# Seven-product down projections in a two-block fp32 kernel, modulation loads issued by GpSimd, and a third buffer of probabilities

## The chip, the cores and the metric

The kernel runs on one core of one Trainium2 chip. The metric is the device time of one execution in microseconds, the median over runs. Everything is fp32.

## The reference, cut to what matters

Two transformer blocks run one after the other on 256 tokens of width 1024, each two layers deep. The change touches the first block's layers and the modulation vectors of the second block's first layer.

```
# first block, for layer in (0, 1)
xn = rms_norm(x, mix_norm[layer])
layer 0: mixed = fox_diff_mixer(...)      # 8 heads of forgetting attention, 4 of differential attention
layer 1: mixed = mlstm_mixer(...)
x = x + mixed
x = x + memory_cross_attention(rms_norm(x), rms_norm(mem), wq, wkv, wo)
h = causal_depthwise_conv(rms_norm(x) @ w_up, conv_w) + conv_b       # 1024 -> 2 x 2816
g, u = split(h);  x = x + (gelu(g) * u) @ w_down                     # 2816 -> 1024
# second block, before its first layer
mod  = silu(c)     @ w_mod[0] + b_mod[0]   # 6144 outputs from 1024 inputs
modc = silu(c_ctx) @ w_mod[0] + b_mod[0]
```

The modulation depends on c and c_ctx alone. It can be computed at any time before the second block.

## The kernel before

**Layout.** Activations are kept feature-major: X, XN and SQ are tiles of 128 features by 8 feature blocks by 512 columns, of which the first 256 are the tokens (T) and the second 256 are free in the first block, apart from keys and values of the memory. A large `arena` is carved into areas by hand. The weights come as one stream of slabs (2 to 2.8 MB each) into two slots; SyncE (SP) issues each slab's DMA when TensorE has finished the slab two before it (L2986). Every engine runs one fixed program, written part by part with `add(...)`; parts of one engine run strictly in the order in which they were added, and semaphores tie the engines together. So where a part stands in VectorE's order decides what waits behind it.

**Order of the stages in the first block, layer 0.** `memkv0` (keys and values of the memory), the norm `mixnorm0`, `foxgate` (forget gates, followed by `add_log_sigmoid` on ScalarE and VectorE and a scan), `foxin` (the input projection: 8 jobs of two 128-feature tiles over 256 tokens, then 4 token-major jobs), `fox` (the attention, `*_pairs`), `subln`, `mixout0`, `xq0`, `xatt0` (cross attention), `xo0`, `fnorm0`, `upa0`, `downa0`. Layer 1 ends likewise with `upa1` and `downa1`; the last layer of the second block ends with `downb1`.

**foxin.** Job j writes PSUM bank j mod 4. ScalarE reads jobs 0, 1, 4, 5; VectorE reads jobs 2, 3, 6, 7 (L2016, L1504). TensorE may start job j only when job j-4 has been read out of its bank (`claim`).

**The up projections** (`*_up_seven`) compute each pair of 128-feature tiles with seven products of quarters in place of eight (Strassen's scheme in Winograd's form), 22 blocks of which 16 run in a hardware loop of 4 turns.

**The down projections.** `downb0` and `downb1` use seven products (`*_down_seven`): for each pair of output tiles, 7 products of 11 k tiles, each over half of the tokens. GpSimd and VectorE form the sums of the weight quarters in the slot, VectorE forms four sums of the hidden activations once. `downa0` and `downa1` use the plain form (`add_out` to `tensor_linear`): 8 output tiles by 22 k tiles over 256 tokens. An fp32 matmul is two matmul instructions in the trace, so the plain form has 352 and the seven-product form 616.

**The modulation** has 48 tiles of 128 outputs. Each tile is a 512 KB piece of w_mod, transposed; VectorE multiplies it with silu(c) and sums along the row (L619, `tensor_tensor_reduce` of 128x1024), once for c and once for c_ctx, so 96 products. Before, 24 tiles are done in `upa0`/`downa0` and 24 in `upa1`/`downa1`: one per turn of the loop, one behind some of the last blocks, six between up and down, and the rest between the reads of the plain down projection. SP issues their loads among the slabs (L2992), with four buffers.

**The forgetting and differential attention** (`*_pairs`) has 8 units (4 pairs of forgetting heads, 4 differential heads). Per unit u: scores on TensorE; `minima(u)` on VectorE, which adds the mask, writes into the probabilities' buffer and takes the minimum; exponentials on ScalarE; `recip(u)`, the scaling (L1463); transposes `turn(u)` on TensorE (L1349); copies; values. VectorE's order is minima(u), recip and scaling of u-1, copy of u-2. There are two buffers, so minima(u) waits for turn(u-2), the last reader of the buffer.

Of the kernel before, what the change touches and what calls it, by code (L numbers as in the profile page):

```python
# [23 lines left out]
P = 128  # L24
# [229 lines left out]
def two_blocks(nc, x_in, mem_in, ctx_in, c_in, small_in, weights_in, mod_in, out, known):  # L254
# [6 lines left out]
    with ExitStack() as ctx:  # L261
# [4 lines left out]
        for n in ("tensor_done", "scalar_done", "vector_done", "gpsimd_done",  # L266
                  "landed0", "landed1", "mod_landed0", "mod_landed1", "mod_landed2", "mod_landed3", "late_landed0", "late_landed1", "loaded_c", "landed_first", "landed_second", "loaded_x", "loaded_mem0", "loaded_mem1", "loaded_mem2", "loaded_mem3", "loaded_ctx", "loaded_small", "loaded_rest",
                  "conv_done", "mod_done", "stored"):
            sems[n] = ctx.enter_context(nc.semaphore(n))
# [3 lines left out]
        CD, MD = "conv_done", "mod_done"  # L273
# [334 lines left out]
        MOD_LOOP, MOD_HALF = 4, MOD_TILES // 2  # L608

        def mod_slot(r):  # L610
            return 0 if r < MOD_LOOP else (r - MOD_LOOP + 1) % 4

        def mod_landed(f, r):

            before = [mod_slot(i) for _ in range(f) for i in range(MOD_HALF)] + [mod_slot(i) for i in range(r + 1)]
            return sems[f"mod_landed{mod_slot(r)}"], 16 * before.count(mod_slot(r))
# [4 lines left out]
        def vector_mod_turn(dve, s, g, turn):  # L621

            f = int(s[1])
            if g == 0:
                sem, landed = mod_landed(f, 0)
                dve.wait_ge(sem, landed + 16 * turn)
                dve.wait_ge(*of(s, "mod_kept", turn=turn, back=1))
            w = mod_slots[0]
            vector_mod_product(dve, w, MODC[:, g, :, :], tiny[:, 48 + g:49 + g], w if g else MODP)\
                .then_inc(*tick(MD, s, "mod_product", g))  # L630
            if g:
                dve.wait_ge(*of(s, "mod_product", 1, turn=turn))
                dve.tensor_copy(MOD[:, 0, bass.ds(turn + MOD_HALF * f, 1), :],
                                tiny[:, 48:50].rearrange("p (m g) -> p m g", g=2)).then_inc(*tick(MD, s, "mod_kept"))

        def vector_mod_tile(dve, s, r, g):
            f = int(s[1])
            w = mod_slots[mod_slot(r)]
            if g == 0:
                dve.wait_ge(*mod_landed(f, r))  # L640
                if r > MOD_LOOP:
                    dve.wait_ge(*of(s, "mod_tile", r - 1, 0))
            vector_mod_product(dve, w, MODC[:, g, :, :], MOD[:, 0, MOD_HALF * f + r, g:g + 1], w if g else MODP)\
                .then_inc(*tick(VD, s, "mod_tile", r, g))
# [169 lines left out]
        def scalar_up_seven(act, s, segs):  # L814
            n, _, centre = conv_spec(s[0], segs)
            h = n // 2
            if s[0] == "a":
                act.wait_ge(sems["loaded_c"], 16 * (int(s[1]) + 1))
                act.activation(MODC, MODC, ACT.Silu).then_inc(*tick(SD, s, "silu_c"))

# [29 lines left out]
        def vector_up_seven(dve, s, norm, segs):  # L850
# [49 lines left out]
            def body(i, turn, m):  # L900
# [111 lines left out]
        def tensor_down_seven(pe, s, pairs, n):  # L1012
# [4 lines left out]
            for p in range(pairs):  # L1017
# [38 lines left out]
                Stream.slab += 1  # L1056

        def vector_down_seven(dve, s, pairs, n, gate):
# [5 lines left out]
            def add_to_x(p, i, g, src):  # L1064
                m = 2 * p + i
                x = X[:, m, g * h:(g + 1) * h]
                return dve.scalar_tensor_tensor(out=x, in0=src, scalar=gate(m, g if n > T else 0), in1=x, op0=ALU.mult,
                                                op1=ALU.add)
# [4 lines left out]
            for p in range(pairs):  # L1073
# [54 lines left out]
                add_to_x(p, 0, 1, ps["p3"]).then_inc(*tick(VD, d, "read", 2 * p, 1))  # L1128

        def gpsimd_down_sums(pool, s, p):  # L1130
# [8 lines left out]
            if p == 0 and s == "b1":  # L1139
                return  # L1140
# [186 lines left out]
        PT = [PTR, RT]  # L1327

        def tensor_pairs(pe, s, units, ready, early=None, late=None):
# [13 lines left out]
            def turn(u):  # L1343
                un = units[u]
                for i in (1, 0):
                    claim(pe, 4 + i)
                    pe.wait_ge(*of(s, "probs", u, i))
                    for a, b in un["blocks"]:
                        mm = pe.transpose(PS[:, 4 + i, b:b + P], PR[:, 2 * (u % 2) + i, a:a + P], ident)  # L1349
# [29 lines left out]
        def scalar_pairs(act, s, units, early=()):  # L1379
            def exps(u):  # L1380
                un = units[u]
                act.wait_ge(*of(s, "min", u))
                if u >= 2:
                    act.wait_ge(*of(s, "turned", u - 2, 0))
                if u >= RING:
                    act.wait_ge(*of(s, "rec", u - RING))
                src = PS if un["rows"][0][2] is None else PR
                for i in range(2):
                    for j, (c0, c1, _) in enumerate(un["rows"]):
                        r = i * len(un["rows"]) + j  # L1390
                        op = act.activation(PR[:, 2 * (u % 2) + i, c0:c1], src[:, 2 * (u % 2) + i, c0:c1], ACT.Exp,
# [29 lines left out]
        def vector_pairs(dve, s, units):  # L1421
            def minima(u):
# [4 lines left out]
                if units[u]["rows"][0][2] is not None:  # L1427
                    if u >= 2:
                        dve.wait_ge(*of(s, "turned", u - 2, 0))
# [51 lines left out]
        def gpsimd_pairs(pool, s, units):  # L1481
            if s in ("fox", "batt0", "batt1"):
                return
# [1814 lines left out]
```

## Time and profile before

| | |
|---|---|
| median of 3 runs | 2523.35 us (2518.7 to 2523.64) |
| the profiled execution, its own time | 2517.16 us |
| its span | 2515.1 us |
| instructions | 36,716 |
| TensorE busy | 98% of the span |
| weights and other reads from memory | 331.72 MB, mean 132 GB/s |

The profile is one execution taken by the hardware profiler. Times in it are microseconds from the span's start. PE is TensorE's matmuls, PEld its weight loads, DVE is VectorE, ACT ScalarE, POOL GpSimd, SP SyncE. Matmuls are pipelined, and the end of a group is modelled, so distances between the starts of groups are read rather than durations. "idle before <- releaser" is the time the engine stood still before an instruction and who ended that. PEclk is the granted TensorE clock, where 1.00 is 2.4 GHz and 0.50 is 1.2 GHz.

### The profile page before, as it was taken

To read this page: it belongs to the slowest core of one execution; us is meant where nothing else is said; L and a number is where in the kernel's file an instruction comes from. 1 tells how busy PE (TensorE), PEld (TensorE's weight loads), DVE (VectorE), ACT (ScalarE), POOL (GpSimd) and SP (SyncE) were. 2 spreads that over 40 slices of the span, in tenths; PEclk is the share of its full clock that TensorE was granted. 3 is DMA by queue.
4 is the path that set the end of the run, shared out by engine and by line. 5 is a ranking of instruction groups with operands and counts; after the bars stand their busy time and mean duration, and the time that the engine had idled before them with its cause. 6 is when DMAs were issued, how large, how long until landed. Compare 5 with 4: busy or idle time off the path is not lost.

```text
span 2515.1 us, 36716 instructions
## 1 busy us (share of the span) xinstructions
PE 2475.1 (98%) x14000; PEld 2020.7 (80%) x14000; DVE 1270.1 (51%) x2602; ACT 544.5 (22%) x1198; POOL 550.1 (22%) x474
## 2 busy tenths in 40 slices
PE   9989999999999999999999999999999999999999
PEld 6857899986799998745567666888888875999999
DVE  3034178751325887324846763544542247435774
ACT  1131122111212220213630001222200215212220
POOL 1000135200212540001002321323241010232543
PEclk9999999999999999999999999999999999999999
DMA  6323265643334566121023662121222120243453
GB/s 236 134 101 117 84 226 186 261 180 134 117 134 168 193 226 234 67 81 39 1 84 142 222 252 104 67 100 67 113 92 80 67 94 26 104 167 150 167 193 109
DMA packets 40018, 334.59 MB, mean 133 GB/s; under 512 B 3920, under 2 KB 10192, under 8 KB 22736
## 3 DMA queue, kind: packets, MB, share of 16 engines
q1 hardware_dynamic: 39888, 332.78, 35.7%
q8 instruction: 91, 1.49, 0.2%
q14 instruction: 39, 0.32, 0.0%
HBM read 331.72 MB, written 1.05 MB: 132 GB/s over the span
## 4 chain that ended last, share of the span: by engine, by line
PE 92%; DVE 3%; DMA 3%; POOL 1%; ACT 1%; issue 1%; SPq 0%; DVEq 0%; POOLq 0%; ACTq 0%
PE PS L769 25%; PE PS L569 21%; PE PS L2763 6%; PE PS L1029 6%; PE PS L1529 6%; PE PS L1719 4%; PE PS L2804 4%; PE PS L1338 3%; PE PS L1704 3%; PE PS L2282 2%; PE PS L1349 2%; PE PS L1361 2%; DMA slot<-in_weights 2%; PE PS L436 1%; PE PS L750 1%; PE PS L2420 1%
## 5 line engine op out<-in xcount | busy, mean ns | idle before, releaser
L569 PE MATMUL PS<-XN,slot 128*128 128x256 f32 (+1 forms) x1184 | 296.8, 411 | 0.8 <-DVE XN L508 0.8
L769 PE MATMUL PS<-SQ,slot 128*128 128x128 f32 (+1 forms) x1984 | 294.5, 301 | 2.2 <-DVE slot L865 2.2
L569 PEld LDWEIGHTS PS<-XN,slot 128*128 128x128 f32 x1184 | 224.5, 190 | 69.9 <-issue 42.5
L769 PEld LDWEIGHTS PS<-SQ,slot 128*128 128x128 f32 x1984 | 268.1, 191 | 15.5 <-DVE slot L865 2.6
L769 PE MATMUL PS<-XN,slot 128*128 128x128 f32 (+1 forms) x1664 | 250.0, 301 | 0.0
L569 PE MATMUL PS<-arena,slot 128*128 128x256 f32 x1088 | 236.6, 379 | 0.8 <-DMA slot<-in_weights 0.7
L769 PEld LDWEIGHTS PS<-XN,slot 128*128 128x128 f32 x1664 | 226.1, 192 | 10.7
L569 PEld LDWEIGHTS PS<-arena,slot 128*128 128x128 f32 x1088 | 206.3, 190 | 30.8 <-issue 1.9
L892 DVE SCALAR_TENSOR_TENSOR arena<-PS,small,arena 128x255 f32<-128x255 f32 (+2 forms) x352 | 174.9, 544 | 47.3 <-ACT arena L836 47.1
L836 ACT ACTIVATE arena<-PS,small 128x256 f32<-128x256 f32 (+1 forms) x176 | 105.1, 616 | 376.3 <-DVE PS L925 237.6
L480 POOL TENSOR_TENSOR SQ<-SQ 128x512 f32<-128x512 f32 (+1 forms) x36 | 42.3, 1178 | 536.6 <-ACT SQ L446 536.1
L1029 PE MATMUL PS<-arena,slot 128*128 128x128 f32 (+1 forms) x846 | 130.6, 314 | 1.3 <-DVE arena L1103 0.8
L1029 PEld LDWEIGHTS PS<-arena,slot 128*128 128x128 f32 x846 | 119.9, 191 | 10.0 <-DVE arena L1103 1.0
L446 ACT ACTIVATE SQ<-X 128x512 f32<-128x512 f32 (+1 forms) x68 | 36.2, 551 | 410.3 <-DVE X L1642 172.2
L619 DVE CUSTOM_DVE_ANT_1 arena<-arena 128x1024 f32<-128x1024 f32 x96 | 121.2, 1312 | 3.7 <-DMA arena<-in_mod 3.7
L2763 PE MATMUL PS<-arena,slot 128*128 128x256 f32 (+1 forms) x704 | 119.6, 328 | 1.5 <-DVE slot L2887 1.4
L2763 PEld LDWEIGHTS PS<-arena,slot 128*128 128x128 f32 x704 | 107.0, 191 | 11.6 <-DVE slot L2887 2.2
L769 PE MATMUL PS<-SQ,probs 128*128 128x128 f32 (+1 forms) x704 | 111.4, 301 | 1.3 <-DVE SQ L877 1.3
L1719 PE MATMUL PS<-arena,slot 128*128 128x128 f32 (+1 forms) x688 | 110.1, 321 | 0.0
L950 POOL TENSOR_TENSOR slot<-slot 128x512 f32<-128x512 f32 x84 | 109.0, 1297 | 0.0
L1719 PEld LDWEIGHTS PS<-arena,slot 128*128 128x128 f32 x688 | 101.4, 191 | 8.4 <-issue 0.5
L962 POOL TENSOR_TENSOR arena<-arena 128x256 f32 (+3 forms) x88 | 79.8, 906 | 113.7 <-ACT arena L845 113.7
(291 smaller groups left out, 3661.8 us busy)
## 6 DMA issues: line engine op xcount, KB each, us to landing
slot<-in_weights SPq DMA_DIRECT2D x85, 2048.0 KB, 7.8
arena<-in_mod SPq DMA_DIRECT2D x96, 512.0 KB, 3.4
slot<-in_weights SPq DMA_DIRECT2D x16, 2816.0 KB, 9.7
slot<-in_weights SPq DMA_DIRECT2D x24, 1536.0 KB, 6.7
slot<-in_weights SPq DMA_DIRECT2D x5, 1024.0 KB, 4.8
slot<-in_weights SPq DMA_DIRECT2D x2, 2176.0 KB, 8.8
arena<-in_c SPq DMA_DIRECT2D x3, 1024.0 KB, 10.9
small<-in_small SPq DMA_DIRECT2D x1, 1982.0 KB, 17.2
```

The costliest lines, as they stand in the source:

```text
L569: mm = pe.matmul(o, l, r, start=k == 0, stop=k == len(terms) - 1, skip_group_check=True)
L619: return dve.tensor_tensor_reduce(scratch, w, c, 1.0, 0.0, ALU.mult, ALU.add, total)
L769: mm = pe.matmul(PS[:, bank, 0:h], lhs[:, k * P:(k + 1) * P], rhs(k), start=first and k == 0, stop=last and k == 3, skip_group_check=True)
L836: act.activation(hb[:, half, :], src[half], ACT.Identity, bias=conv_col(s, m - 1, half, 3), scale=conv_col(s, m - 1, half, centre))\
L892: op = dve.scalar_tensor_tensor(out=o[:, :, lo:hi], in0=x[:, :, lo + d:hi + d], scalar=conv_col(s, m - 1, half, c), in1=o[:, :, lo:hi], op ...
L950: pool.tensor_tensor(a21, a11, a21, ALU.subtract).then_inc(*w_tick(s, GD, "s3", i, turn))
L962: pool.tensor_tensor(dst, hb[:, 0, :], hb[:, 1, :], ALU.mult).then_inc(*w_tick(s, GD, "h", i, turn))
L1029: mm = pe.matmul(d_psum(p, what, h), lhs[:, k * P:(k + 1) * P], rhs(k), start=k == 0, stop=k == KH - 1, skip_group_check=True)
L1529: mm = pe.matmul(PS[:, bank, 0:cols_n], lhs(k, t), r, start=k == 0, stop=k == k_tiles - 1)
L1719: mm = pe.matmul(PS[:, bank_of(m), part[g]], w[:, a:a + P], rhs(k, part[g]), start=k == 0, stop=k == k_tiles - 1, skip_group_check=True)
L2763: mm = pe.matmul(PS[:, bank, 0:hq], lhs[:, k * P:(k + 1) * P], rhs[:, k, 0:hq], start=first and k == 0, stop=last and k == 3, skip_group_c ...
L2804: mm = pe.matmul(PS[:, BBR + i, 0:nq], slot[:, a:a + P], BR[b][:, k, 0:nq], start=k == 0, stop=k == 3, skip_group_check=True)
```

## The change

1. `downa0` and `downa1` use `*_down_seven`, with half the tokens (128 columns) per product, as `downb1` does. Nothing is gated there, so the addition to X is a plain addition. The context norm that was laid behind the first job of `downa1` is now laid behind its second pair.
2. All 48 modulation tiles move to layer 0 of the first block: tiles 0 to 7 right before `foxgate`'s read, 8 to 15 before the read of `foxin` job 2, 16 to 22 before that of job 6, 23 to 32 before the attention, 33 to 39 between the reads of `mixout0`, 40 to 47 between those of `xo0`. They have three buffers. Their loads are issued by GpSimd, each when the tile three before it is done, and no longer by SP. silu(c) is computed before tile 0 (in the free half of X) and once more before tile 40. The products inside the up stages and their loads between slabs are gone.
3. The attention `fox` has three buffers of probabilities: minima(u) waits for turn(u-3).

```diff
-        MODC = H[:, 0:DK, T:2 * T].rearrange("p (g j) t -> p g j t", g=2)
-        MODP = H[:, DK:DK + 4, T:2 * T]
-        mod_slots = [area(15360 + D * i, 4, T) for i in range(4)]
+        MODC = [X[:, :, T:2 * T].rearrange("p (g j) t -> p g j t", g=2), area(12288, 2, 4, T)]
+        mod_slots = [[area(at, 4, T) for at in (16384, 17408, third)] for third in (12288, 14592)]
+        MODP = area(18432, 4, T)
...
+        MOD_SLOTS, MOD_OUT, MOD_XO = 3, 35, 40
+        def vector_mod_tiles(dve, *tiles):
+            for n in tiles:
+                w = mod_slots[n >= MOD_OUT][n % MOD_SLOTS]
+                c = MODC[n >= MOD_XO]
+                if n in (0, MOD_XO):
+                    dve.wait_ge(*of("silu_c", int(n >= MOD_XO)))
+                dve.wait_ge(sems[f"mod_landed{n % MOD_SLOTS}"], 16 * (n // MOD_SLOTS + 1))
+                for g in range(2):
+                    if g == 0 and n:
+                        dve.wait_ge(*of("mod_tile", n - 1, 0))
+                    vector_mod_product(dve, w, c[:, g, :, :], MOD[:, 0, n, g:g + 1], w if g else MODP)\
+                        .then_inc(*tick(VD, "mod_tile", n, g))
+                if n % MOD_HALF == MOD_HALF - 1:
+                    vector_mod_end(dve, 0, n // MOD_HALF, [("mod_tile", n, 1)])
+        def gpsimd_mod_loads(pool, tiles):
+            for n in tiles:
+                if n == 2:
+                    pool.wait_ge(*of("memkv0", "job", 3))
+                if n == MOD_OUT:
+                    pool.wait_ge(*of("subln", "out", 3, 0))
+                if n >= MOD_SLOTS:
+                    pool.wait_ge(*of("mod_tile", n - MOD_SLOTS, 1))
+                pool.dma_start(mod_slots[n >= MOD_OUT][n % MOD_SLOTS], mod_in[n].rearrange("p (j t) -> p j t", t=T))\
+                    .then_inc(sems[f"mod_landed{n % MOD_SLOTS}"], 16)
+        def scalar_silu_c(act, f):
+            act.wait_ge(sems["loaded_c"], 16 * (f + 1))
+            act.activation(MODC[f], MODC[f], ACT.Silu).then_inc(*tick(SD, "silu_c", f))
...
-                if s[0] == "a" and turn is not None:
-                    if i == 0:
-                        dve.wait_ge(*of(s, "silu_c"))
-                    if i % 2 == 0:
-                        vector_mod_turn(dve, s, i // 2, turn)
-                elif s[0] == "a" and i >= W_LAST and i % 2 == 0:
-                    vector_mod_tile(dve, s, MOD_LOOP, (i - W_LAST) // 2)
...
-            if p == 0 and s == "b1":
+            if p == 0 and s != "b0":
                 return
...
+        PAIR_SETS = {t: [PR[:, 0:2, :], PR[:, 2:4, :]] for t in ("fox", "batt0", "batt1")}
+        PAIR_SETS["fox"].append(area(18432, 2, 512))
...
-                if u >= 2:
-                    act.wait_ge(*of(s, "turned", u - 2, 0))
+                if pair_before(s, u) >= 0:
+                    act.wait_ge(*of(s, "turned", pair_before(s, u), 0))
...
-            add_out(f"d{s}", lambda k: H[:, k, 0:T * len(segs)], None, FM, segs, gate,
...
+            add(tensor=lambda pe: tensor_down_seven(pe, s, DK // 2, n, tensor_then),
+                vector=lambda d: vector_down_seven(d, s, DK // 2, n, gate, vector_then),
+                gpsimd=lambda p: gpsimd_down_seven(p, s, DK // 2, n))
...
+                add(scalar=lambda a: scalar_silu_c(a, 0), vector=lambda d: vector_mod_tiles(d, *range(0, 8)),
+                    gpsimd=lambda p: gpsimd_mod_loads(p, range(0, MOD_OUT)))
...
+                def vector_foxin(dve, jobs=fox_jobs):
+                    for j, job in enumerate(jobs):
+                        vector_mod_tiles(dve, *{2: range(8, 16), 6: range(16, 23)}.get(j, ()))
+                        reads_linear(dve, VD, "vector", "foxin", [job], j)
+                    vector_mod_tiles(dve, *range(23, 33))
...
                 add_out("mixout0", lambda k: O1[:, k, :],
...
+                        [(33, 34), (35, 36, 37), (38, 39), ()])
...
+                add_out("xo0", lambda k: O1[:, k, :], lambda k: ("xatt0", "out", k // 2), DK, [0],
+                        [(40, 41, 42), (43, 44, 45), (46, 47), ()])
...
+            prev_ready = [[(f"da{l}", "read", 2 * p, 1)] for p in range(DK // 2)]
...
+                if g == 2:
+                    load_c(0)
+                if g == first_slab["mixout0"] + 1:
+                    sp.wait_ge(*of("subln", "out", 3, 0))
+                    load_c(1)
```

## Rows read from the trace of the kernel before

**Rows 1.** The page: busy time by engine; GpSimd's busy tenths in 40 slices
```profile
PE 2475.1 (98%) x14000; PEld 2020.7 (80%) x14000; DVE 1270.1 (51%) x2602; ACT 544.5 (22%) x1198; POOL 550.1 (22%) x474
...
POOL 1000135200212540001002321323241010232543
```

**Rows 2.** The page: the chain that ended last, shares by engine
```profile
PE 92%; DVE 3%; DMA 3%; POOL 1%; ACT 1%; issue 1%; SPq 0%; DVEq 0%; POOLq 0%; ACTq 0%
```

**Rows 3.** Waits of PE: total us, times, longest
```profile
PE PS L1349 <- DVE probs L1463: 6.1, 5, 1.6
...
PE PS L769 <- DVE slot L865: 2.2, 2, 1.1
```

**Rows 4.** PE in order: start, us, instructions, [idle before]
```profile
69.40 55.52 PE L569 MATMUL PS<-XN,slot 128*128 128x256 f32 x256
...
458.55 3.84 PE L769 MATMUL PS<-SQ,slot 128*128 128x128 f32 x32 [1.07 <-DVE slot L865]
...
470.26 76.14 PE L569 MATMUL PS<-arena,slot 128*128 128x256 f32 x352
...
2440.75 5.08 PE L1029 MATMUL PS<-arena,slot 128*128 128x128 f32 x44
...
2454.93 10.09 PE L1029 MATMUL PS<-arena,slot 128*128 128x128 f32 x88 [0.79 <-DVE arena L1103]
...
2501.71 9.99 PE L1029 MATMUL PS<-arena,slot 128*128 128x128 f32 x88
```

**Rows 5.** The chain that ended last, 440 to 475: start, us
```profile
444.11 8.92 DMA slot<-in_weights
```

**Rows 6.** DVE in order, foxgate to fox, then products and a read
```profile
69.50 0.47 DVE L2002 TENSOR_SCALAR arena<-PS,small 8x256 f32<-8x256 f32 x1 [1.21 <-PE PS L569]
...
73.17 0.68 DVE L2009 TENSOR_TENSOR_SCAN arena<-small,arena 8x256 f32<-8x256 f32 x1
...
118.05 0.69 DVE L1504 COPY arena<-PS 128x512 f32<-128x512 f32 x1 [20.03 <-PE PS L569]
...
156.24 0.29 DVE L1432 CUSTOM_DVE_ANT_0 probs<-PS,small 128x128 f32<-128x128 f32 x1 [30.59 <-PE PS L1338]
...
509.06 1.21 DVE L619 CUSTOM_DVE_ANT_1 arena<-arena 128x1024 f32<-128x1024 f32 x1
...
510.20 2.29 DVE L619 CUSTOM_DVE_ANT_1 arena<-arena 128x1024 f32<-128x1024 f32 x1
```

**Rows 7.** POOL in order, 505 to 512
```profile
509.89 1.52 POOL L480 TENSOR_TENSOR SQ<-SQ 128x512 f32<-128x512 f32 x1 [35.51 <-ACT SQ L446]
```

**Rows 8.** ACT in order, at 67 and at 799
```profile
67.75 0.17 ACT L1932 ACTIVATE tiny<-PS 128x2 f32<-128x2 f32 x1
...
70.89 1.28 ACT L3108 ACT_TABLE_LOAD   x1
...
799.12 1.91 ACT L819 ACTIVATE arena<-arena 128x2048 f32<-128x2048 f32 x1 [6.94 <-DMA arena<-in_c]
```

**Rows 9.** The page: DMA issues, KB each, us from issue to landing
```profile
slot<-in_weights SPq DMA_DIRECT2D x85, 2048.0 KB, 7.8
arena<-in_mod SPq DMA_DIRECT2D x96, 512.0 KB, 3.4
```

**Rows 10.** Windows: length, busy us by engine, PEclk, DMA share, GB/s
```profile
core 0: us, PE busy (x) PEld busy (x) DVE busy (x) ACT busy (x) POOL busy (x), PEclk, DMA share, GB/s
169.64:173.21 3.57, 2.58 (x26) 1.62 (x26) 2.76 (x14) 2.34 (x10) 0.00 (x0) 1.00 0.00 0
173.21:177.05 3.84, 2.58 (x26) 1.63 (x26) 2.99 (x15) 2.72 (x11) 0.00 (x0) 1.00 0.00 0
...
325.00:328.00 3.00, 0.50 (x3) 0.30 (x2) 2.96 (x4) 0.00 (x0) 2.74 (x2) 1.00 0.68 169
330.00:333.00 3.00, 3.00 (x16) 2.95 (x15) 2.89 (x5) 0.00 (x0) 0.00 (x0) 0.50 0.96 376
333.00:336.00 3.00, 3.00 (x27) 3.00 (x27) 1.98 (x4) 0.00 (x0) 0.00 (x0) 0.95 1.08 383
10.00:20.00 10.00, 9.99 (x46) 8.48 (x46) 3.43 (x5) 3.88 (x7) 3.26 (x3) 1.00 1.05 414
```

More of the change, by code:

```diff
@@ L605, in conv_spec @@
             return n, taps, centre
[L608 to L616, printed above, removed]
+        MOD_HALF = MOD_TILES // 2
+        MOD_SLOTS, MOD_OUT, MOD_XO = 3, 35, 40
         def vector_mod_product(dve, w, c, total, scratch):
@@ L1056, in tensor_down_seven, with vector_down_seven @@
                 Stream.slab += 1
-        def vector_down_seven(dve, s, pairs, n, gate):
+                if then and p == 1:
+                    then(pe)
+        def vector_down_seven(dve, s, pairs, n, gate, then=None):
             h, d = n // 2, f"d{s}"
@@ L1066, in add_to_x @@
                 x = X[:, m, g * h:(g + 1) * h]
+                if gate is None:
+                    return dve.tensor_tensor(x, src, x, ALU.add)
                 return dve.scalar_tensor_tensor(out=x, in0=src, scalar=gate(m, g if n > T else 0), in1=x, op0=ALU.mult,
@@ L2039, in two_blocks @@
                 add(scalar=lambda a: scalar_memory_values(a, 0))
+                add(scalar=lambda a: scalar_silu_c(a, 1), gpsimd=lambda p: gpsimd_mod_loads(p, range(MOD_OUT, 43)))
                 add_out("mixout0", lambda k: O1[:, k, :],
-                        lambda k: ("fox", "out", 3) if k < 4 else ("subln", "out", k - 4, 0), DK, [0])
+                        lambda k: ("fox", "out", 3) if k < 4 else ("subln", "out", k - 4, 0), DK, [0],
+                        [(33, 34), (35, 36, 37), (38, 39), ()])
             else:
@@ L2219, in two_blocks @@
             if l == 0:
-                add_out("xo0", lambda k: O1[:, k, :], lambda k: ("xatt0", "out", k // 2), DK, [0])
+                add(gpsimd=lambda p: gpsimd_mod_loads(p, range(43, MOD_TILES)))
+                add_out("xo0", lambda k: O1[:, k, :], lambda k: ("xatt0", "out", k // 2), DK, [0],
+                        [(40, 41, 42), (43, 44, 45), (46, 47), ()])
                 units = norm_x(s, X, XN, lambda m, g: col("ffn_norm0", m), after_out("xo0", [0], None), [0])
@@ L3040, in _ @@
                             load(g0 + j, n // P // P, src[turn * 2 + j])
-                            if s[0] == "a" and j == 0:
-                                sp.wait_ge(*of(s, "mod_product", 1, turn=turn, back=1))
-                                load_mod(int(s[1]), 0, turn)
                     g = g0 + 2 * W_TURNS
-                    if s[0] == "a":
-                        for rs in ((7,), (), (8,), range(9, 15), range(15, 18), range(18, MOD_HALF)):
-                            sp.wait_ge(*slot_free(g))
-                            load(g, len(table[g][1]), piece(g))
-                            g += 1
-                            for r in rs:
-                                sp.wait_ge(*(of(s, "mod_product", 1, turn=W_TURNS - 1) if r == 7 else
-                                             of(s, "mod_tile", r - 4, 1)))
-                                load_mod(int(s[1]), r)
                     continue
```

142 lines of the change are left out of this document (37 added, 105 removed).

## The prediction

> **What bounds the kernel now.** The busy line first: TensorE works 98% of the span, the next engine 51% [rows 1]. The chain of work that ended last is TensorE for 92% [rows 2]. So only two things move the time: fewer TensorE microseconds, and stalls of TensorE, of which the list of waits has few; the largest is the transposes' wait in the forgetting attention, 6.1 us in five waits [rows 3]. VectorE is half idle over the span, but a part that stands in its fixed order can hold back a read for which a PSUM bank is waiting, and that must be read stage by stage.
>
> **Down projections.** Plain: 352 matmul instructions of 256 columns without a gap, from 470.26, 76.14 us [rows 4]; `downa1` is the same. The seven-product form with the same shapes is already there as `downb1`: from 2440.75 to 2501.71 + 9.99 = 2511.70, 70.95 us [rows 4]. That is not seven eighths of 76.14 (66.6), for two reasons that the rows show. A plain instruction costs 76.14/352 = 0.216 us for 256 columns, and one of 128 columns costs (2511.70 - 2454.93)/506 = 0.112 us (506 instructions remain from 2454.93: 23 products of 22), a bit more than half; so 616 x 0.112 = 69.1. And the first pair waits for VectorE's sums, the last time 0.79 us [rows 4], in all 70.95 - 69.1 = 1.9 us. In `downa` VectorE has the same chain of sums ahead of it, and no modulation products any more. Gain 5.2 us each, 10.4 for both; bounds 7.1 each (no stall) and 3 each (stall doubled). GpSimd's sums of weights lie beside TensorE as in `downb1`. The last addition to X shrinks from 512 to 128 columns; only behind `downa1` does a norm wait for it: -0.3.
>
> **Up projections.** The products leave VectorE and their loads leave SP's queue. TensorE's wait at 458.55 is 1.07 us [rows 4]; it goes back to a slab that took 8.92 us to land [rows 5] where the median is 7.8 [rows 9], beside a modulation load. I take -1.1; `upa1` has nothing comparable in its first blocks but a small wait behind the load of c, -0.2. Late next is nothing: the other blocks run without gaps. Bounds 0 and 2.2 [rows 3].
>
> **Third buffer.** The cycle before is turn(u-2), minima(u), scaling(u-1), turn(u-1): 3.57 us per unit, 3.84 with a differential head, while VectorE works 2.76 and 2.99 of it and stands idle 0.81 and 0.85 [rows 10]. With the third buffer minima(u) need not wait for turn(u-2), and VectorE itself becomes the bound. The first four units have no gap on TensorE, so nothing is won there. TensorE waits in five periods [rows 3]. Each loses VectorE's idle time but for some 0.17 that I leave for the signals between engines, my choice: 5 x 0.66 = 3.3 us. Bounds 0 (another wait takes its place) and 6.1 [rows 3].
>
> **The 33 products' tiles before the attention.** This is where the change costs. A product's pitch is 510.20 - 509.06 = 1.14 us [rows 6], a tile has two, 2.29. VectorE's order is now: tile 0 can begin when silu(c) is there. ScalarE ends the exponential at 67.92, loads a table (1.28), and computes 128x2048 in 1.91 [rows 8]: 71.1. Then, with p the time of a tile:
> - eight tiles, 8p; the gate's read, log-sigmoid and scan, 69.50 to 73.85 = 4.35 [rows 6]; eight tiles, 8p; the read of job 2, 0.69.
> - TensorE begins job 6 of `foxin` at 69.40 + 6 x 6.92 = 110.9 (256 instructions in 8 jobs, 55.4 us) [rows 4], but its bank is that of job 2. It waits until 71.1 + 16p + 5.0: a stall of 16p - 34.8.
> - Down to the attention VectorE has 33 tiles and four reads: free at 78.1 + 33p; before, its first minimum was at 156.24 [rows 6]. The shift is 33p - 78.1 if that is larger.
>
> At p = 2.29, with every load early, the stall is 1.9 us: it can't be avoided, since VectorE is now the bound of the stage. The loads set p. A tile is 524 KB per 2.29 us, 229 GB/s, and a slab 2.1 MB per 13.8 us, 152: 381 together, where the window from 10 to 20 us moved 414 [rows 10]. So they fit just so, but compete: while a slab is on its way (2.1 MB at half of 414: 10.1 of each 13.8 us) a tile's bytes need 2.53 us, else 2.29 counts; 10.1/2.53 + 3.7/2.29 = 5.6 tiles in 13.8 us, p = 2.46. Stall 4.6 us (the other shift is 3.1, smaller). ScalarE sits behind the gate as well: job 0 is read only after 8p, at about 95, before job 4 wants the bank at 97.1; that cover is gone from p = 2.75.
> The clock: after 325 to 328, where TensorE worked 0.50 of 3 us, it was granted 0.50, the lower of its two levels, in 330 to 333 and 0.95 to 336, 1.65 us lost [rows 10]. A stall of 4.6 us is longer than that gap, so I add 1.65; below, 0. Sum of the stage: +6.2, bounds +1.9 and the rivals'.
> GpSimd's issuing costs nothing in itself: it computes next to nothing in the second to fourth of the page's slices, 63 to 252 us [rows 1]. Queued behind its waits are the norm sums of `xnorm0` and `fnorm0`, which are wanted after the last tile is done. No row has a load issued by GpSimd; the nearest is SP's, 3.4 us from issue to landing [rows 9]. With three buffers a load has 2 x 2.29 = 4.58 us, so 1.2 us are to spare; a landing time L beyond 4.58 gives p = (L + 2.29)/3.
> The Trainium skill (DMA: Bandwidth & Descriptors, Latency and other measured facts) gives the first byte about 1 us from GpSimd against 0.6 from SP; an estimate from that is L = 3.8, still within the 4.58, and the sum by it is the same.
>
> **Tiles 33 to 47.** Seven between the reads of `mixout0` and eight in `xo0`: 16.0 and 18.3 us of VectorE under 27.7 us of TensorE each, none before the last read. A product beside a GpSimd sum took 2.29 in place of 1.21 us [rows 6, 7]; that happens twice there and stays hidden. 0.
> SP's new wait for `subln` stands behind a slab already issued: 0.
>
> **Sum.** -10.4 - 0.3 - 1.3 - 3.3 + 6.2 = -9.1 us on the profiled execution's 2517.16, so 2508.1; the median of the runs lies 6.2 higher, 2523.35 - 9.1 = 2514.3.
>
> **Rivals.**
> 1. The loads keep up and the short stall leaves the clock: +1.9 in place of +6.2, in all -13.4, 2510.0. For it: 414 GB/s against 381.
> 2. The third buffer only moves the wait (ScalarE has 2.3 to 2.7 us per unit and copies of its own): 3.3 less, -5.8, 2517.6.
> 3. GpSimd's issuing and the products take turns. Rows 6 and 7 show a product held for a whole GpSimd sum. If each issue waits for a running product, L grows by up to 1.14: 3.4 + 1.27 (half the rate) + 1.14 = 5.8, p = 2.70, shift 33 x 2.70 - 78.1 = 11.0, and 1.65: in all -2.6, 2520.7, no change that can be told.
>    The Trainium skill (SBUF — State Buffer, Who interferes with whom) says that descriptors of a GpSimd-issued DMA are held up by VectorE copies in a 2-port mode, and that an operation with two SBUF inputs holds up only GpSimd's reads, which speaks against this rival: nearly all work here is products with two inputs or copies out of PSUM. By that rule the sum is the forecast's.
> 4. The other side: a load issued by GpSimd lands in twice SP's time, 6.8 us. p = 3.03, shift 21.9, + 1.65 - 15.3 = +8.2, 2531.6. It decides from p = 2.79 (L = 6.1), where gain and cost are equal. For it: nothing in the trace tells L; against it: the spare 1.2 us.
>
> **Chances.** Forecast 0.42, rival 1 0.23, rival 2 0.10, rival 3 0.17, rival 4 0.08. 0.2% (5 us) is what a measurement of this kernel can tell from no change. Faster: forecast, 1 and 2 short of 0.03 near the bound, 0.72; same: rival 3 and that rest, 0.20; slower 0.08. The range goes from rival 1 less a spread of runs of 2.5 us, 2507.5, to rival 3, 2521.
>
> **What would show it.** The two down stages at about 71 us each with three short waits in the first pair; the wait at L865 in `upa0` gone; a stall of TensorE before job 6 of `foxin`, behind VectorE's read of job 2, and its length is 16p - 34.8; product pitch 1.14 and idle of VectorE on the modulation's DMA; turn waits in `fox` down from 6.1 to about 3. The prediction is wrong if p leaves 2.29 to 2.7, or if slabs land late because the modulation's loads take more than half of the DMA engines.

## The result, and the profile after

The kernel after takes 2524.83 us (median of 20 runs, 2518.03 to 2531.53), the kernel before 2521.45 in the same sessions (20 runs, 2517.68 to 2527.25). The ratio is 1.0015, with a 95% interval from 1.0008 to 1.0022: slower by some 3.8 us, within 0.2% for most of the interval, where 9 us less were forecast. The profiled execution of the kernel after took 2524.87 us with a span of 2523.1, that of before a span of 2515.1. So the two profiles stand 8.0 us apart and the ratio says 3.8: the profiled execution of before, 2517.16 us, was faster than any of its 20 runs. Differences between stages below are of the two profiles; of the time as a whole the ratio counts.

The page of the kernel after: its busy lines, the chain by engine and the tiles' issues (beside [rows 1, 2, 9]):

```profile
PE 2467.7 (98%) x14528; PEld 2029.7 (80%) x14528; DVE 1334.9 (53%) x2707; ACT 548.2 (22%) x1200; POOL 623.4 (25%) x536
...
PE 88%; DVE 5%; DMA 3%; issue 2%; ACT 1%; POOL 1%; SPq 0%; DVEq 0%; POOLq 0%
...
arena<-in_mod POOLq DMA_DIRECT2D x48, 512.0 KB, 5.6
arena<-in_mod SPq DMA_DIRECT2D x48, 512.0 KB, 3.3
```

TensorE is 88% of the chain instead of 92%, and a tile that GpSimd issues lands in 5.6 us (median of 48). SyncE's 48 tiles in the last line are those of the second block's second layer, a later stage. What the same 48 tiles took before, when SyncE issued them (L2992), and what they take now (L637), least, median and most:

```profile
DMA to landing us min/median/max: 3.0/4.6/13.7
```

```profile
DMA to landing us min/median/max: 3.3/5.6/11.6
```

The waits of TensorE, then of VectorE from 60 to 180 us (total, times, longest), beside [rows 3]:

```profile
PE PS L1339 <- DVE pair_min L1434: 8.5, 1, 8.5
PE PS L569 <- DVE arena L1496: 5.3, 1, 5.3
...
PE PS L1016 <- DVE arena L1083: 2.7, 3, 2.0
...
PE PS L767 <- DVE slot L859: 1.7, 1, 1.7
```

```profile
DVE arena L612 <- DMA arena<-in_mod: 19.5, 5, 4.8
```

The turn wait that led the list before (6.1 us) is off its top; two waits for VectorE took its place, and VectorE in its turn stood 19.5 us waiting for tiles. TensorE in order, at the points that answer to [rows 4]:

```profile
69.88 41.71 PE L569 MATMUL PS<-XN,slot 128*128 128x256 f32 x192
116.93 16.28 PE L569 MATMUL PS<-XN,slot 128*128 128x256 f32 x64 [5.35 <-DVE arena L1496]
133.05 27.63 PE L1521 MATMUL PS<-slot,XN 128*128 128x512 f32 x64
...
175.75 0.80 PE L1339 MATMUL PS<-arena 64*128 64x128 f32 x4 [8.49 <-DVE pair_min L1434]
...
485.46 5.08 PE L1016 MATMUL PS<-arena,slot 128*128 128x128 f32 x44
490.37 2.62 PE L1016 MATMUL PS<-arena 128*128 128x128 f32 x22
493.09 2.69 PE L1016 MATMUL PS<-arena,slot 128*128 128x128 f32 x22
496.17 2.69 PE L1016 MATMUL PS<-arena,slot 128*128 128x128 f32 x22 [0.38 <-DVE arena L1083]
499.58 10.09 PE L1016 MATMUL PS<-arena,slot 128*128 128x128 f32 x88 [0.73 <-DVE arena L1094]
...
556.19 3.62 PE L569 MATMUL PS<-XN,slot 128*128 128x256 f32 x16
...
2448.70 5.08 PE L1016 MATMUL PS<-arena,slot 128*128 128x128 f32 x44
```

Read each start against the same point of the kernel before and the time can be followed through the program. `foxin` begins 0.48 us late. The forgetting attention ends, and the norm behind it begins, 15.7 us late (205.76 against 190.06). `upa0` gives 0.5 back, so `da0` begins at 485.46 for 470.26, 15.2 late. `da0` gives 5.25 back (556.19 for 546.24), `upa1` 0.6, `da1` 2.3, 7.05 us stay. In the second block, where the change touches nothing, the distance still wanders: 7.04 at 1314, 8.97 at 1514, 9.35 at 2310 us; `db1` begins 7.95 us late, at 2448.70 for 2440.75. But for the 0.9 us of the second block, all of the loss lies ahead of 206 us.

VectorE where the attention begins, beside [rows 6]:

```profile
169.81 1.23 DVE L612 CUSTOM_DVE_ANT_1 arena<-arena,X 128x1024 f32<-128x1024 f32 x1 [3.23 <-DMA arena<-in_mod]
...
173.26 1.22 DVE L612 CUSTOM_DVE_ANT_1 arena<-arena,X 128x1024 f32<-128x1024 f32 x1
...
174.40 0.29 DVE L1434 CUSTOM_DVE_ANT_0 probs<-PS,small 128x128 f32<-128x128 f32 x1
```

Its first minimum is at 174.40, 18.16 us later than in the kernel before, straight behind the last product of tile 32. The products' pitch is 1.15 us, as forecast; VectorE's idle time between them is waiting for tiles.

### The profile page after: what moved, and what is told of

The parts are those of the page before. It is cut to its first block, busy times and chain, and to the rows that moved or that the text cites. A ratio compares the mean times of both kernels' runs of the same rounds, so it can differ in the third digit from the quotient of the medians.

```text
span 2523.1 us, 37954 instructions
## 1 busy us (share of the span) xinstructions
PE 2467.7 (98%) x14528; PEld 2029.7 (80%) x14528; DVE 1334.9 (53%) x2707; ACT 548.2 (22%) x1200; POOL 623.4 (25%) x536
## 4 chain that ended last, share of the span: by engine, by line
PE 88%; DVE 5%; DMA 3%; issue 2%; ACT 1%; POOL 1%; SPq 0%; DVEq 0%; POOLq 0%
PE PS L767 25%; PE PS L569 12%; PE PS L1016 11%; PE PS L2737 7%; PE PS L1521 4%; PE PS L1681 4%; PE PS L2778 4%; PE PS L1339 3%; PE PS L1666 3%; DMA arena<-in_mod 2%; PE PS L2256 2%; PE PS L1362 2%; PE PS L1350 2%; DVE arena L612 1%; PE PS L436 1%
## 5 line engine op out<-in xcount | busy, mean ns | idle before, releaser
L1016 PE MATMUL PS<-arena,slot 128*128 128x128 f32 (+1 forms) x1902 | 252.8, 294 | 5.6 <-DVE arena L1083 2.7
L1016 PEld LDWEIGHTS PS<-arena,slot 128*128 128x128 f32 x1902 | 240.6, 193 | 15.2 <-DVE arena L1083 3.2
L612 DVE CUSTOM_DVE_ANT_0 arena<-arena 128x1024 f32<-128x1024 f32 x80 | 106.9, 1376 | 30.1 <-DMA arena<-in_mod 30.0
L2737 PEld LDWEIGHTS PS<-arena,slot 128*128 128x128 f32 x704 | 107.0, 191 | 11.8 <-DVE slot L2861 2.5
L2882 POOL TENSOR_TENSOR slot<-slot 128x512 f32<-128x512 f32 x22 | 29.8, 1353 | 332.8 <-DMA slot<-in_weights 332.8
L1681 PE MATMUL PS<-arena,slot 128*128 128x128 f32 (+1 forms) x688 | 110.1, 321 | 0.0
L937 POOL TENSOR_TENSOR slot<-slot 128x512 f32<-128x512 f32 x84 | 108.6, 1292 | 0.0
L1681 PEld LDWEIGHTS PS<-arena,slot 128*128 128x128 f32 x688 | 101.4, 191 | 8.4 <-issue 0.5
L612 DVE CUSTOM_DVE_ANT_1 arena<-arena,X 128x1024 f32<-128x1024 f32 x80 | 92.6, 1219 | 27.3 <-DMA arena<-in_mod 24.5
L767 PEld LDWEIGHTS PS<-SQ,probs 128*128 128x128 f32 x704 | 97.7, 191 | 6.0 <-DVE SQ L871 1.5
```

The costliest lines, as they stand in the source:

```text
L612: return dve.tensor_tensor_reduce(scratch, w, c, 1.0, 0.0, ALU.mult, ALU.add, total)
L767: mm = pe.matmul(PS[:, bank, 0:h], lhs[:, k * P:(k + 1) * P], rhs(k), start=first and k == 0, stop=last and k == 3, skip_group_check=True)
L937: pool.tensor_tensor(a21, a11, a21, ALU.subtract).then_inc(*w_tick(s, GD, "s3", i, turn))
L1016: mm = pe.matmul(d_psum(p, what, h), lhs[:, k * P:(k + 1) * P], rhs(k), start=k == 0, stop=k == KH - 1, skip_group_check=True)
L1681: mm = pe.matmul(PS[:, bank_of(m), part[g]], w[:, a:a + P], rhs(k, part[g]), start=k == 0, stop=k == k_tiles - 1, skip_group_check=True)
L2737: mm = pe.matmul(PS[:, bank, 0:hq], lhs[:, k * P:(k + 1) * P], rhs[:, k, 0:hq], start=first and k == 0, stop=last and k == 3, skip_group_c ...
```

## The experiments

Each ran against the kernel before on the same chip (median there 2521.91, 2521.83 and 2521.27 us in the three groups of runs).

**The third buffer, taken out of the kernel after and put alone into the kernel before.**

```
-        PAIR_SETS["fox"].append(area(18432, 2, 512))
```

> The kernel after with the forgetting attention's probabilities in two buffers again; all else stays. My theory: the third buffer gives what its step promised. The turn waits of TensorE in that attention are 1.7 us in the kernel after and were 6.1 us before, so without it they come back by 3 to 4 us: 2528.3 us beside the kernel after's 2524.8. Rival: it only moved the waits, and the time stays within 1 us of the kernel after's.

> The kernel before with the third buffer of probabilities and nothing else. My theory: the turn waits fall from 6.1 us to about 2, and the time by 3.5 to 4.5 us, to 2518. Rival: the gain seen so far needs the late start of the attention, and alone it is under 1 us.

Without it the kernel after takes 2529.51 us (1.0038, 1.0025 to 1.005), 4.7 more; alone in the kernel before it gives 2518.07 (0.9989, 0.9979 to 0.9998), 3.8 less. TensorE's waits for turned probabilities, with the buffer in the kernel before alone:

```profile
169.30 0.92 PE L1358 MATMUL PS<-small,arena 128*128 128x128 f32 x6 [0.21 <-DVE arena L1473]
174.97 0.92 PE L1358 MATMUL PS<-small,probs 128*128 128x128 f32 x6 [0.39 <-DVE probs L1473]
177.94 0.92 PE L1358 MATMUL PS<-small,arena 128*128 128x128 f32 x6 [0.39 <-DVE arena L1473]
180.91 0.92 PE L1358 MATMUL PS<-small,probs 128*128 128x128 f32 x6 [0.72 <-DVE probs L1473]
```

1.7 us for 6.1. The gain is there in either setting, and the rival is out. The profile without the buffer shows something more. Its program is the same up to the attention, and VectorE's first minimum came at 173.38 us, near the 174.40 of the kernel after. But two waits for tiles, 5.41 and 4.78 us, fell ahead of the read of job 2 instead of one, so TensorE stood 12.09 us before job 6, and the wait of 8.5 us in the attention was not there. So in this profile the norm behind the attention begins only 0.65 us later than with the buffer (206.41 for 205.76), and the 4.7 us are of the medians. How the delay is split between the two stalls differs between profiles of the same code; the start of the attention differs less (173.4 to 176.7 us in four of them).

**The down projections as plain products again**, in the kernel after: `add_linear` over 22 input tiles in place of `tensor_down_seven` and its sums.

> The kernel after with downa0 and downa1 as plain products again (352 instructions of 256 columns each). From the two traces da0 gained 5.25 us and da1 2.7 with the norm behind it, so my theory is 8 us above the kernel after's 2524.8, 2532.8. Rival: with the slabs of the down projections free earlier or later the stages beside them change too, and the difference is under 5 or above 11 us.

2534.19 us (1.0058, 1.0044 to 1.0072): 9.4 above the kernel after, with `da0` back at one run of 352 instructions in 76.14 us. Its own wait in the attention was 10.60 us for 8.49, and in its profile the norm behind the attention began 1.6 us later (207.40 for 205.76). Taken off, that leaves 7.8 of the 9.4 beside the 7.6 (5.25 and 2.3) that the two profiles show for the stages; medians that come from different executions don't agree more closely than that.

**The context norm's sums on GpSimd**, moved behind its weight sums of `da1`'s second pair:

```
             for p in range(1, pairs):
                 gpsimd_down_sums(pool, s, p)
+                if then and p == 1:
+                    then(pool)
```

> The kernel after, but GpSimd's sums of squares for the context norm come behind its weight sums of da1's second pair instead of ahead of the first pair's end. My theory: VectorE's three sums beside them took 2.69, 2.69 and 2.14 us where da0 shows 1.61 each, which makes TensorE's waits in da1's first pair 3.16 us against 1.11 and costs its clock another 1.3; with the sums moved da1 looks like da0 and the time is 3 to 3.5 us below 2524.8. Rival: the longer sums have another cause, or the moved work makes a later pair wait as long, and the time stays within 1 us.

VectorE in the kernel after, from 939 to 960 us, and GpSimd beside it; then VectorE with the sums moved:

```profile
945.61 2.69 DVE L1075 TENSOR_TENSOR arena<-arena 128x1408 f32<-128x1408 f32 x1
948.22 2.69 DVE L1080 TENSOR_TENSOR slot<-arena,slot 128x1408 f32<-128x1408 f32 x1
950.83 2.14 DVE L1083 TENSOR_TENSOR arena<-arena 128x1408 f32<-128x1408 f32 x1
```

```profile
944.17 5.26 POOL L480 TENSOR_TENSOR SQ<-SQ 128x512 f32<-128x512 f32 x2
949.51 1.99 POOL L487 TENSOR_TENSOR SQ<-SQ 128x256 f32<-128x256 f32 x1
```

```profile
945.71 1.61 DVE L1075 TENSOR_TENSOR arena<-arena 128x1408 f32<-128x1408 f32 x1
947.25 1.61 DVE L1080 TENSOR_TENSOR slot<-arena,slot 128x1408 f32<-128x1408 f32 x1
948.78 1.61 DVE L1083 TENSOR_TENSOR arena<-arena 128x1408 f32<-128x1408 f32 x1
```

The same three sums take 7.5 us beside GpSimd's and 4.8 without. `da1` up to the stage behind it went from 77.52 us (939.69 to 1017.21) to 74.20 (939.79 to 1013.99), 3.3 less, as expected. The whole time was 2523.42 us (1.0008, 0.9999 to 1.0016), 1.4 under the kernel after, and the two intervals overlap, so the runs by themselves don't tell this gain from none; the stage's 3.3 us is read from the two profiles. In this one the waits ahead of the attention were 1.3 us longer (9.2 and 5.9 us), and the norm behind it began 0.6 us later. The Trainium skill (SBUF — State Buffer, Who interferes with whom) says that a VectorE instruction with two SBUF inputs contends with a GpSimd instruction that reads SBUF; the trace agrees: with GpSimd's sums gone from beside it, VectorE's sum takes 1.61 us instead of 2.69.

**Who issues the tiles: ScalarE, or SyncE in the slabs' own queue.** Tiles 3 to 34, each behind the same tile as before:

```
+                        gpsimd_mod_loads(act, {1: range(11, 19), 5: range(19, MOD_OUT)}.get(j, ()))
```
```
+                gpsimd_mod_loads(sp, {1: range(3, 8), 2: range(8, 12), 3: range(12, 18), 4: range(18, 26),
+                                      5: range(26, 32), 6: range(32, MOD_OUT)}.get(g - first_slab["foxin"], ()))
```

> The kernel after, but tiles 3 to 34 of the modulation are issued by ScalarE instead of GpSimd, each at the same condition (the tile three before it is done). My theory: a load that GpSimd issues while a slab is on its way lands only with the slab's end, and this makes a tile 2.85 us instead of 2.29. Then a load from ScalarE, which is treated as SP's are, lands in 3.3 to 4.5 us, the tile takes 2.3 to 2.5 us, TensorE's stall before job 6 of the projections is 2 to 5 us, the wait of 8.5 us at the third unit of the attention falls under 1 us, and the time is 9 to 11 us below the kernel after's, about 2514.8. Rival: it is the DMA engines' share and not the issuer that sets the landing; then tiles stay at 2.8 to 2.9 us and the time within 2 us of 2524.8.

> The kernel after, but tiles 3 to 34 are issued by SyncE, in one queue with the slabs, four to eight behind each slab. My theory: in one queue a load stands behind the whole slab issued just before it, so the first load behind a slab lands some 6 to 8 us after its issue, as with GpSimd, and the time stays within 3 us of the kernel after's 2524.8; a slab never shares the engines, so it lands in under 7 us. Rival: the issuer alone matters, SyncE's loads land in 3.4 us as they did in the kernel before, and the time falls by 9 to 11 us.

Both times came out against my theory. ScalarE: 2527.51 us (1.002, 1.0009 to 1.0031). SyncE: 2515.45 (0.9976, 0.9966 to 0.9987). VectorE's waits for tiles, 60 to 180 us, with ScalarE and with SyncE as the issuer:

```profile
DVE arena L617 <- DMA arena<-in_mod: 19.1, 5, 4.7
```

```profile
DVE arena L617 <- DMA arena<-in_mod: 11.0, 4, 4.7
```

The kernel after has 19.5 us, ScalarE as the issuer 19.1 and SyncE 11.0: so it isn't GpSimd. ScalarE's kernel has a fault of its own, too: its token copies stand behind its last loads, and TensorE waited 15.4 us for them; the waits for tiles don't hang on that. With SyncE the stall before job 6 was 6.5 us, the wait of 8.5 in the attention was gone. What SyncE has and the other two have not is one queue for tiles and slabs, or the order that goes with it: there a slab is issued only behind the tiles that stand ahead of it.

**Queue or order.** The kernel after with GpSimd's loads, and each slab held until the tile behind which SyncE had issued it:

```
+                behind = {2: 4, 3: 8, 4: 14, 5: 22, 6: 28}.get(g - first_slab["foxin"])
+                if behind:
+                    sp.wait_ge(*of("mod_tile", behind, 1))
```

> The kernel after, with GpSimd's loads, but SyncE issues five of the slabs no earlier than it did where it issued the tiles too: each waits for the tile that is three before the last load ahead of it there. It tells the queue from the order. Theory order: the loads by SyncE gained because a slab stood back behind the tiles wanted first; then the time is near 2515.5 here too. Theory queue: a load in a queue of its own needs some 3.5 us to its first packet beside a slab and gets a fifth of the rate, whatever is held back; then the time stays above 2521.

2525.21 us (1.0019, 1.0011 to 1.0028), waits for tiles 20.4 us. By the numbers that I had set this is the theory of the queue, but the rows don't bear it out, because the edit didn't give SyncE's order. Tile 17 and the slab beside it, with SyncE as the issuer of both, then in this run:

```profile
115.60 0.33 SPq L642 DMA_DIRECT2D arena<-in_mod  x1
115.97 0.43 SPq L2965 DMA_DIRECT2D slot<-in_weights  x1
```

```profile
114.10 0.33 SPq L2960 DMA_DIRECT2D slot<-in_weights  x1
114.32 0.53 POOL L637 DMA_DIRECT2D arena<-in_mod  x1 [1.76 <-DVE modulation L612]
```

Slab and tile wait for the same product here, and the slab gets away 0.2 us ahead of the tile that SyncE had put before it. That tile then took 8.8 us to land. It was so with the next two held slabs too, and the seventh slab, which stood behind tile 34 with SyncE, wasn't held at all. Where the order was the same, at the slab of 98 us, the tile behind it took 9.2 us in SyncE's one queue and 7.8 in a queue of its own. And with either queue VectorE's waits end at the same distance from a slab's issue: 9.1 to 10.4 us in the kernel after, 9.5 to 10.4 with SyncE, 9.3 to 10.1 with ScalarE. So the rows speak for the order: with SyncE one tile more is on its way before each slab, and fewer slabs fall into the stretch. No run has that order with two queues, so it isn't shown.

**Packets.** The transfers of the kernel after between 100 and 102 us, then between 103 and 105 (queue: packets, MB, share of the 16 engines; q1 carries the slab issued at 97.80, q0 the tiles issued at 99.19 and 101.48):

```profile
q1 hardware_dynamic: 51, 0.84, 98.7%
q0 software_dynamic: 7, 0.01, 1.6%
```

```profile
q1 hardware_dynamic: 41, 0.67, 78.5%
q0 software_dynamic: 38, 0.16, 18.9%
```

```
+                for q in range(4):
+                    sem = f"landed{g % 2}" if q == 3 else f"quarter_landed{g % 2}"
+                    sp.dma_start(slots[g % 2][:, q * 1024:(q + 1) * 1024], src[:, q * 1024:(q + 1) * 1024])\
```

> The kernel after, but each of six slabs that are loaded beside the tiles is issued as four loads of 1024 columns, so that its packets are 4 KB long like the tiles' and not 16 KB; issuer, order and bytes stay. Theory one, formed after the loads by ScalarE fared as GpSimd's and those in SyncE's own queue better: an engine serves two queues packet by packet, so beside 16 KB packets a tile's 4 KB packets get a fifth of the rate (83 of 414 GB/s, 6.3 us for 524 KB), and beside 4 KB packets half (2.5 us). Then a tile issued in a slab's flight lands in 4 to 5 us, VectorE's waits for tiles fall from 19.5 us to under 9, TensorE's wait of 8.5 us in the attention to under 3, the slabs land in about 10 us, and the time is 6 to 10 us below 2524.8. Rival: the second queue waits for the slab whatever its packets (order, or a fixed priority), and waits and time stay within 2 us.

2524.96 us (1.001, 1.0 to 1.002; one of its 11 runs, 9869.5 us, stands apart and is unexplained). From 104 us the two queues did move 0.19 and 0.19 MB in a microsecond, so the sharing by packets is real. But the first tile still moved nothing from 100 to 103 us, and the slab, with half of the rate, was on its way until 108: the bytes queued together are the same. VectorE's waits for tiles were 18.5 us. My theory that the share was the cost is out.

**The slabs' bytes.** Only a quarter of each slab is loaded beside the tiles:

```
+                elif g in quarter:
+                    load(g, 8, piece(g)[:, 0:8 * P])
```

> The kernel after, but of each of the six slabs loaded beside the tiles only the first quarter of the columns is loaded (512 KB in place of 2 MB), so three quarters of those weights are old data; all instructions stay. My theory: the waits for tiles come from the slabs' bytes. Then tiles follow each other at 2.29 us, VectorE's waits for tiles fall from 19.5 us to under 3, the stall before job 6 is 1.9 us (16 x 2.29 - 34.8), the wait of 8.5 us in the attention is gone, and the time is some 15 us below the kernel after's 2524.8, near 2510. Rival: GpSimd's issuing itself is slow beside VectorE's products; then the waits stay above 12 us and the time within 5 us of 2524.8.

2511.25 us (0.9969, 0.9954 to 0.9984), 13.6 under the kernel after. VectorE's and TensorE's waits:

```profile
DVE arena L612 <- DMA arena<-in_mod: 2.5, 5, 1.0
```

```profile
PE PS L569 <- DVE arena L1496: 2.7, 1, 2.7
```

The waits for tiles fell from 19.5 to 2.5 us, the stall before job 6 was 2.7, the wait of 8.5 gone. GpSimd issued all the tiles just as before. These quarters have 4 KB packets too, but the run before had those with all the bytes and gained nothing. So the slabs' bytes are what the tiles wait for.

**Fewer tiles ahead of the attention, and reads that don't stand behind them.** Nine tiles go beside `xq0`, where VectorE worked 0.83 us of the 28 from 262 to 290; then the reads of jobs 2 and 3 go behind tile 11 instead of 15, and GpSimd's norm sums are moved as above.

```
-                [(33, 34), (35, 36, 37), (38, 39), ()])
+                [(24, 25), (26, 27, 28), (29, 30), ()])
...
+                add(vector=lambda d: vector_mod_tiles(d, *range(31, 40)), gpsimd=lambda p: gpsimd_mod_loads(p, range(34, 43)))
```
```
-  {2: range(8, 16), 6: range(16, 23)}
+  {2: range(8, 12), 6: range(12, 20)}
```

> The kernel after with 24 instead of 33 tiles ahead of the attention; seven in the output projection behind it, nine beside the query projection of the cross attention, where VectorE has next to nothing to do for some 34 us, and eight in xo0. My theory: the wait of 8.5 us before the third unit of the attention and the clock's loss behind it go away, the stall before job 6 (5.35 us) stays, the rest is hidden: 10 us less than the kernel after, 2514.8. Rival: the nine tiles hold back something in the cross attention or its keys and 3 us or more come back there: 2518 or above.

> Nine tiles later as in the run of that name, the context norm's sums later, and in the projections ahead of the attention VectorE's reads of jobs 2 and 3 stand behind 12 tiles instead of 16, with the rest behind them. My theory: the stall of 5.4 us before job 6 and the 2.4 us of clock behind it go, the norm gives 3.3: 11 us below that run's 2514.0, 2503. Rival: the tiles now hold the read of job 6 and a token product waits instead; then 2508 or above.

2514.03 us (0.9969, 0.9959 to 0.9979) with nine tiles moved; 2504.23 (0.9935, 0.9923 to 0.9947) with all three, the fastest kernel here: by the ratios some 16 us under the kernel before and 20 under the one after. TensorE through `foxin` and to the attention in that last kernel:

```profile
69.88 55.52 PE L569 MATMUL PS<-XN,slot 128*128 128x256 f32 x256
125.24 27.63 PE L1523 MATMUL PS<-slot,XN 128*128 128x512 f32 x64
```

No gap, 55.52 us as in the kernel before. VectorE still waits 16.7 us for tiles in this stretch, but no instruction of TensorE's waits for these products, so it costs nothing.

## Why the prediction was wrong

**The step that failed** is the loads' rate: "while a slab is on its way (2.1 MB at half of 414: 10.1 of each 13.8 us) a tile's bytes need 2.53 us, else 2.29 counts", so p = 2.46 us. Slab and tile don't get halves here. The slab's bytes come first, all but whole: the tile issued 1.4 us behind the slab moved nothing for 3.6 us, then a fifth of the rate, and landed after 7.8 us, and three buffers hold 2 x 2.29 us of cover. VectorE waited five times, and the waits ended 9.2, 10.2, 9.4, 10.4 and 9.1 us behind a slab's issue (the first two at 107.02 and 121.83 us, slabs issued at 97.80 and 111.62). Measured over 33 tiles with the shift formula: (174.40 - 78.1)/33 gives p = 2.92, the start 0.5 us later in it; from the waits alone it is 2.29 + 19.5/33 = 2.88. Either is outside the 2.29 to 2.7 that I had set as the limits of the prediction.

**What went in wrong.** The other half of that step is L. I took SyncE's 3.4 us [rows 9] as the landing of a tile and found 1.2 us to spare. That row is the median of 96 tiles, and half of them are the second block's, which land in 3.3 us; for the 48 tiles of this change the same trace has 4.6, and up to 13.7. With 4.6 nothing is to spare.

**What followed from it.** The formula of the first stall held. It was 5.35 us; 16p - 34.8 needs 2.51 for that, and the first 16 tiles, into which only the first of the five waits falls, took 2.29 + 3.54/16 = 2.51 each. The shift before the attention, forecast 3.1 and "smaller", was 18.2 and became the one that counts. That 33p - 78.1 gives 18.2 tests nothing, since p = 2.92 comes from it; with the 2.88 from the waits it gives 16.9. I had compared the two branches at a single p, a mean over the period of a slab: 381 of 414 GB/s is no reserve when a load may start only after a product.

**The clock.** Forecast 1.65 us once. The windows of the kernel after (length, busy by engine, PEclk, DMA share, GB/s):

```profile
113.00:116.00 3.00, 0.00 (x0) 0.00 (x0) 3.00 (x5) 0.00 (x0) 0.53 (x1) 0.76 0.77 299
116.00:119.00 3.00, 2.07 (x5) 1.71 (x6) 1.48 (x4) 0.00 (x0) 0.53 (x1) 0.50 0.95 381
119.00:122.00 3.00, 3.00 (x10) 2.41 (x9) 0.17 (x1) 0.00 (x0) 0.00 (x0) 0.60 0.98 397
...
175.00:178.00 3.00, 2.25 (x10) 1.83 (x12) 2.15 (x17) 2.37 (x11) 0.00 (x0) 0.50 0.10 41
178.00:181.00 3.00, 3.00 (x10) 1.88 (x9) 0.86 (x5) 1.25 (x6) 0.00 (x0) 0.50 0.00 0
181.00:184.00 3.00, 3.00 (x18) 2.07 (x16) 2.65 (x14) 2.35 (x9) 0.00 (x0) 0.69 0.00 0
```

Each of the two long stalls was followed by a stretch at 0.50 of the full clock. The first cost 2.3 us (64 instructions from 116.93 to 133.05, 16.1 us where 64 of 256 take 13.8), but in the shadow of the second, since VectorE was behind anyway. The second is paid: from the first minimum to the norm 31.36 us in place of 33.82 (156.24 to 190.06), 2.5 less, where the third buffer alone takes 4.4 of waits away; some 1.9 were lost. So the stage costs 18.2 + 1.9 before the buffer's gain, against 6.2. By the two profiles the whole is then 20.1 - 4.4 (buffer) - 7.6 (down projections) - 1.1 (up projections) + 0.9 (second block) = 7.9 us, where the ratio says 3.8.

**Down projections**: forecast -10.4 and -0.3. `da0` gave 5.25 us, with waits of 0.38 and 0.73, as the prediction had it (5.2). `da1` gave 2.3 with the tail; the sentence "GpSimd's sums of weights lie beside TensorE as in `downb1`" looked only at the weights' sums. Another sum of GpSimd's, the context norm's, stood beside VectorE's chain and lengthened it by 2.7 us; waits of 1.18 and 1.98, and a clock of 0.54 in the next window. With it moved the stage took 3.3 less.

**Up projections**: forecast -1.3, measured -1.1. The wait of 1.07 us at 458.55 is gone, but the same statement (L865 before, L859 after) now makes TensorE wait 1.68 us at 373.70, earlier in `upa0`.

**Third buffer**: forecast -3.3; measured 3.8 alone, 4.7 taken out of the kernel after. VectorE's idle time went almost whole: with the buffer alone the units follow each other at 2.97 us instead of 3.57 to 3.84. Rival 2 is out.

**Tiles 33 to 47**: forecast 0, measured 0: the offset is 15.7 us at 206 us and still so at 305.

**The rivals.** Rival 1 needed loads that keep up, and rival 3 a slow issue; with the slabs' bytes gone, GpSimd's issues of 0.53 us each and the products ran side by side without loss, so rival 3's mechanism isn't there. Rival 4 came nearest: its p of 3.03 and shift of 21.9 us stand beside 2.92 and 18.2. By the time alone, 2524.83 us, rival 3's 2520.7 is nearer than rival 4's 2531.6. Rival 4 had the wrong cause (the issuer, at all times) for the right sign, and I gave it 0.08 with the words "nothing in the trace tells L". The trace of before told both sides: the slab of 8.92 us [rows 5] beside one tile, 1.1 more than the median, and the tiles' own 4.6.

**Still open.** Why SyncE's issuing leaves 11.0 us of waits instead of 19.5 is argued, not shown: the rows speak for the order of tiles and slabs and against the queue, since where the order was equal the one queue landed the tile later (9.2 for 7.8 us). A kernel with GpSimd's loads in which each slab waits until the tile ahead of it has been issued would settle it. What makes the pause of over 3 us isn't settled either; it is there with GpSimd and with ScalarE as the issuer, and with either packet length of the slab.

## What to carry to other kernels

When small loads run beside large ones, in one queue or in two, work out how many buffers cover the large load's whole flight; that bytes per microsecond fit isn't enough. Read the time to landing from the loads in question and not from a median over all loads of that name. Where an engine's fixed order mixes filler with reads that free a PSUM bank, put the reads ahead of as much filler as the bank allows, and keep filler out of the stretch ahead of a stage that this engine leads: here both, with the norm's sums moved, were worth some 20 us. When VectorE takes over a chain that TensorE waits for, look at every operation of GpSimd's beside it, not only those of the same stage.

## What the runs showed of the hardware

- A 512 KB load in a second queue, issued 1.4 us behind a 2 MB load, had no packets for 3.6 us (1.2 us for the one issued 0.9 us ahead of the slab) and landed after 7.8 us (3.9 for that one). Issued by ScalarE, 1.9 us behind its slab, it had none for 3.5 us and landed after 7.4. In SyncE's queue, 1.1 us behind the slab, it landed after 9.2.
- With any of the three, VectorE's waits for tiles ended 9.1 to 10.4 us behind a slab's issue.
- Two queues share the engines by packets: 41 and 38 packets in 2 us, 0.67 and 0.16 MB; with 4 KB packets on both sides 0.19 and 0.19 MB in a microsecond.
- VectorE sums of 128x1408 with two SBUF inputs took 2.69 us beside GpSimd sums, 1.61 without.
- TensorE idle from 111.6 to 116.93 us: the granted clock was 0.50, the lower of its two levels, from 115 to 121 us, and 1.00 from 122. Idle from 167.3 to 175.75: 0.50 from 170 to 182, and 1.00 from 183. So it fell inside the gap, and came back some 4.5 and 7 us after TensorE had begun again.
